# A streaming encoder layer on one Trainium2 core: seven block products for the first token group's last sixteen gate-up slabs

## The chip, the cores and the metric

One core of one Trainium2 chip runs the whole kernel as one program. The metric is the device time of one execution in microseconds; lower is better. Engines: TensorE (PE), VectorE (DVE), ScalarE (ACT), GpSimd (POOL), and SyncE (SP), which only issues DMAs here. ACT issues DMAs too.

## The reference, cut to what matters

One encoder layer is computed for 2048 prompt tokens and 32 sample tokens, D_MODEL = 1024, D_FF = 2816. The last part, which the change touches, is

```python
x = layer_norm(ALPHA * x + g1 * mix_out, ln1_g, ln1_b)
h = layer_norm(x) * (1.0 + sc2) + sh2
gu = h @ w_gu                                    # (tokens, 2 * D_FF)
ff = (silu(gu[..., :D_FF]) * gu[..., D_FF:]) @ w_down
x = layer_norm(ALPHA * x + g2 * ff, ln2_g, ln2_b)
```

Everything is float32. The kernel makes each float32 operand of these products from two float16 parts, a high and a low one, and sums three matmuls (high x high, high x low, low x high: `TERMS`).

## The kernel before, in words

The stages follow one another: projections, attention, the mixer's output (stage D, which leaves h in `hidden_t` as high and low halves), then stage E, gate-up and down. Stage E takes the tokens in three groups of 768, 768 and 544, and each group as two halves (384, 384, 272 columns). The 2816 hidden channels are 22 slabs (`NF`) of 128. For each slab j PE computes gate and up for both halves; ACT and DVE make silu(gate) * up; its high half is written by ACT, its low half by POOL, into `E_HID`. After 22 slabs come two down passes of three tiles of 128 tokens (`down`, line 2470 on).

**Groups two and three** compute a slab by seven block products (`product`, 2436 on; matmul line 2457). [gate; up] and the two halves of the 1024 input channels make a 2 x 2 block problem over the two token halves; with sums of weight blocks and sums of token blocks it takes 7 products of 12 matmuls, 84, in place of 8, 96. The results are combined by ACT (`copy1` to `copy3`, `sigmoid1`, `sigmoid2`, 1293 to 1322; high halves, 1327) and DVE (`gate1`, `gated1`, `up2`, `hidden2`, `hidden1`, 1928 to 1958). PE's order is 2, 6, 5, 7 of slab j, 1 of slab j + 1, 4 and 3 of slab j. Product 7 waits for the copy after 6, 4 for the copy after 7, 3 for `up2`. `copy2` waits for POOL's low half of the slab before, since its buffer holds the hidden part until then.

**Group one** (`gate_up`, 2413 on; matmul line 2426) computes each slab by plain products, 96 matmuls: blk 0 and blk 1, gate and up, 48 matmuls for each blk. Beside it, it prepares what groups two and three read:

- SP loads a slab of `w_gu` (1 MB float32) into one of two homes (`load_gu`, 688).
- ACT writes its high half (`gu_split`, 1264), DVE the low half (`gu_low`, 1878), into `E_GHL`.
- POOL makes four weight sums of 512 columns (`weight_sums`, 922 to 928) into `E_TSUM`; ACT and DVE split them (`sum_split`, 1272; `sum_low`, 1885) into `E_THL`, a single buffer.
- SP stores three blocks of 256 KB and the sums, 1 MB, to `gs_dram` (`store_gs`, 729 to 738), from where groups two and three load them.
- `hidden` (ACT 1282, 1284; DVE 1918, 1921; POOL's `lo_hid`, 942) makes the slab's hidden values, one blk after the other, with one float32 buffer `E_H` between them. PE's next slab waits for `hid_set` of the slab before, blk by blk.

Nothing is scheduled by a planner: each engine's order is written out by hand in its own loop over j, with semaphore waits. Slab 0's weights are split in stage D before its sums are due, so slab 0 is loaded and summed again in mid-stage as slab `NF` (`T_MID` = 11, `RAW_ORDER`). Two gate rows for the end (`gate_turn2`, 2467: PE; `gate_rows`, 1345: ACT) are made during slabs 1 and 2.

**Between the groups** POOL makes the next group's token sums (`token_sums`, 954 on, instructions at 964, 970, 972) while PE runs the down passes. In group one's first down pass ACT and DVE also split the 22 down slabs (`dn_split`, 1338; `dn_low`, 1964) and SP stores them one after the other (791), each store after the landing of the one before.

Of the kernel before, what the change touches and what calls it, by code (L numbers as in the profile page):

```python
# [57 lines left out]
def encoder_step(nc, x_prompt, x_sample, cache_k, cache_v, state_pool, c_prompt, c_sample,  # L58
# [5 lines left out]
    with ctx:  # L64
# [131 lines left out]
        E_GRAW = [w32(22576, 2048), w32(16896, 2048)]  # L196
# [153 lines left out]
        T_MID = NF // 2  # L350
        RAW_ORDER = [*range(T_MID + 1), NF, *range(T_MID + 1, NF)]
        RAW_POS = {m: at for at, m in enumerate(RAW_ORDER)}

        def graw_home(m):
            return E_GRAW[0 if m == 0 or RAW_POS[m] % 2 else 1]

        def raw_in(m):
            at = RAW_POS[m]
            home1 = at and at % 2 == 0
            return gu_raw[1 if home1 else 0], 32 * (at // 2 if home1 else (at + 3) // 2 if at else 1)  # L360

        def std_n(n):
            return 5 * n - 3 + 4 * (n > T_MID) if n else 1

        def sum_n(m, i):
            return (5 * T_MID + 2 if m == NF else 5 * m - 2 + 4 * (m > T_MID)) + i

        def stored_n(m):
            return 48 + 64 * (T_MID if m == NF else m) + 16 * (m > T_MID)

        ALL_STORED = 64 * NF

        GS_STEPS = [(1, 0)] + [(q, j + (q == 1)) for j in range(NF) for q in (2, 6, 5, 7, 1, 4, 3)
                               if (q, j) != (1, NF - 1)]
        MM_AT = (2 * NF, 9 * NF, 16 * NF)
        GS_MM = {key: at + 1 for at, key in enumerate(GS_STEPS)}

        def product_n(grp, q, j):
            return MM_AT[grp - 1] + GS_MM[q, j]

        def copy_n(grp, c, j):
            return 3 * NF * (grp - 1) + 3 * j + c

        def add_n(grp, a, j):
            return 2 * NF * (grp - 1) + 2 * j + a
# [78 lines left out]
        def _(sp):  # L464
# [39 lines left out]
            sp.dma_start(ln2_rows[:, 0, :], ln2_g[0:1, :].partition_broadcast(P)).then_inc(ln_in, 16)  # L504
            sp.dma_start(ln2_rows[:, 1, :], ln2_b[0:1, :].partition_broadcast(P)).then_inc(ln_in, 16)
# [191 lines left out]
            for t in range(14):  # L697
# [4 lines left out]
                if t == 12:  # L702
                    sp.wait_ge(gu_lo, 1)
                    load_gu(1)
# [11 lines left out]
            def next_gu(m):  # L716
                if m == 2:
                    sp.wait_ge(d_mm, NT + 1)
                    sp.wait_ge(d_x1, NT + 1)
                else:  # L720
                    gone = RAW_ORDER[RAW_POS[m] - 2]
                    if gone < NF:
                        sp.wait_ge(gu_lo, std_n(gone))
                    sp.wait_ge(t_sum, 4 * RAW_POS[gone])
                load_gu(m)
# [7 lines left out]
            def store_gs(m):  # L733
                sp.wait_ge(gu_lo, sum_n(m, 3))
                sp.wait_ge(gs_stored, stored_n(RAW_ORDER[RAW_POS[m] - 1]))
                if m < NF:
                    store_blocks(m)
                sp.dma_start(gs_dram[m % NF, :, 2:6], E_THL).then_inc(gs_stored, 16)

# [21 lines left out]
            for grp in range(3):  # L761
                n0, g0 = 6 * grp, 2 * NF * grp
                for c in range(NF):
                    if grp == 0:
                        if c == 0:
                            store_blocks(0)
                        if c + 2 < NF:
                            next_gu(c + 2)
                        if c + 2 == T_MID:
                            next_gu(NF)  # L770
                        if c + 1 < NF:
                            store_gs(c + 1)
                        if c + 1 == T_MID:
# [1777 lines left out]
```

## Time and profile before

| what | value |
| --- | --- |
| median of 3 runs | 2582.84 us (2579.41 to 2584.56) |
| the profiled execution | 2587.18 us, span 2585.5 us |
| PE, DVE, ACT, POOL busy | 94%, 55%, 39%, 35% |
| group one, gate-up | 1219.6 to 1575.5 us |
| group one, down | 1575.5 to 1755 us |
| group two, gate-up by seven products | 1755 to 2056 us |

A row of a group gives the engine, the source line, what is written and read with shapes, the count, the busy time, the mean duration, and the idle time of the engine just before with what ended it. In a timeline, each row begins with its start and its duration in microseconds from the start of the span.

### The profile page before, as it was taken

How to read it: one execution, taken by the hardware profiler on the slowest of the kernel's cores; microseconds unless marked ns; L12 is line 12 of the kernel's file. 1: busy time of each engine (PE TensorE's matmuls, PEld its weight loads, DVE VectorE, ACT ScalarE, POOL GpSimd, SP SyncE). 2: the span in 40 equal slices, each digit the busy share in tenths (PEclk: the TensorE clock that was granted, in tenths of full speed). 3: DMA queues.
4: the chain of work that ended last, by engine and by line, in shares of the span. 5: the costliest groups of instructions: out<-in, count | busy, mean ns of one | idle time of the engine just before them, and what ended most of it. 6: DMA issues, size and time to landing. Idle time of an engine off the chain costs nothing.

```text
span 2585.5 us, 36302 instructions
## 1 busy us (share of the span) xinstructions
PE 2431.2 (94%) x14328; PEld 1349.6 (52%) x14328; DVE 1415.9 (55%) x1861; ACT 1018.5 (39%) x1555; POOL 892.8 (35%) x1061
## 2 busy tenths in 40 slices
PE   4899899899998889999999999899999999999998
PEld 3445455444444444454565665345666544688733
DVE  4747665488888887889655554415333302433214
ACT  1522233499999895324443442102222200133200
POOL 1300000277777773333556556501111250111100
PEclk8899999899999999999999999999999999999999
DMA  7315868332332112222556566654454445476555
GB/s 249 100 50 171 283 235 272 120 99 82 99 84 81 34 66 93 78 94 84 165 179 212 179 198 234 227 196 155 155 163 131 139 138 180 153 224 203 186 164 167
DMA packets 216387, 395.63 MB, mean 153 GB/s; under 512 B 30189, under 2 KB 152365, under 8 KB 207642
## 3 DMA queue, kind: packets, MB, share of 16 engines
q1 hardware_dynamic: 199226, 331.45, 40.1%
q10 hardware_dynamic: 16992, 61.87, 7.7%
q8 instruction: 113, 1.85, 0.3%
q14 instruction: 56, 0.46, 0.1%
HBM read 302.97 MB, written 90.30 MB: 152 GB/s over the span
## 4 chain that ended last, share of the span: by engine, by line
PE 58%; DVE 9%; ACT 4%; POOL 4%; DMA 3%; issue 3%; SPq 0%; POOLq 0%; DVEq 0%; ACTq 0%
PE ps L2457 20%; PE ps L2497 15%; PE ps L2426 12%; PE ps L2361 3%; DMA dn_dram<-work 3%; DVE work L1709 3%; PE ps L2236 2%; POOL work L880 2%; PE ps L2213 2%; PE ps L2252 2%; ACT ps L1188 2%; ACT work L1176 2%; DVE work L1866 1%; DVE work L1706 1%; DVE work L1456 1%
## 5 line engine op out<-in xcount | busy, mean ns | idle before, releaser
L2457 PE MATMUL ps<-hidden_t,work 128*128 128x384 f16 (+1 forms) x3696 | 515.2, 303 | 1.9 <-ACT work L1307 1.1
L2497 PE MATMUL ps<-work 128*128 128x512 f16 x2244 | 472.5, 380 | 8.5 <-DVE work L1964 5.9
L2457 PEld LDWEIGHTS ps<-hidden_t,work 128*128 128x128 f16 x3696 | 361.4, 98 | 155.7 <-ACT work L1307 1.7
L2120 PE MATMUL ps<-hidden_t,work 128*128 128x416 f16 x1920 | 353.6, 345 | 14.2 <-DVE hidden_t L1474 10.0
L2426 PE MATMUL ps<-hidden_t,work 128*128 128x384 f16 x2112 | 347.6, 328 | 4.1 <-DVE work L1921 4.1
L2497 PEld LDWEIGHTS ps<-work 128*128 128x128 f16 x2244 | 206.4, 98 | 274.0 <-issue 29.8
L880 POOL TENSOR_TENSOR work<-work 128x512 f32<-128x512 f32 (+2 forms) x320 | 306.8, 965 | 112.4 <-DVE work L1709 63.9
L2426 PEld LDWEIGHTS ps<-hidden_t,work 128*128 128x128 f16 x2112 | 207.5, 98 | 144.3 <-issue 9.6
L2120 PEld LDWEIGHTS ps<-hidden_t,work 128*128 128x128 f16 x1920 | 190.3, 99 | 164.8 <-issue 17.8
L1709 DVE TENSOR_TENSOR_SCAN work<-ps,work 128x512 f32<-128x512 f32 x192 | 237.4, 1270 | 35.2 <-ACT ps L1188 34.3
L841 POOL TENSOR_TENSOR work<-work,col 128x1 f32<-128x1 f32 x68 | 33.2, 488 | 586.2 <-DVE work L1459 586.2
L949 POOL TENSOR_TENSOR work<-work 128x384 f16<-128x384 f32 (+1 forms) x88 | 75.2, 859 | 417.7 <-ACT work L1327 417.7
L2213 PE MATMUL ps<-work 128*128 128x512 f16 (+3 forms) x640 | 175.1, 357 | 37.3 <-DVE work L1709 29.5
L2236 PE MATMUL ps<-ident,work 128*128 128x128 f32 x1088 | 178.4, 280 | 21.8 <-POOL work L880 17.1
L1981 DVE TENSOR_TENSOR work<-ps,work 128x1024 f32<-128x1024 f32 (+1 forms) x17 | 20.8, 1223 | 311.6 <-PE ps L2497 310.3
L2236 PEld LDWEIGHTS ps<-ident,work 128*128 128x128 f32 x1088 | 131.8, 144 | 88.7 <-DVE work L1727 27.9
L1176 ACT ACTIVATE work<-ps,col 128x1024 f32<-128x1024 f32 (+1 forms) x160 | 165.2, 1032 | 8.4 <-PE ps L2213 6.8
L1188 ACT ACTIVATE ps<-ps,col 128x1024 f32<-128x1024 f32 (+1 forms) x160 | 161.5, 1009 | 2.1
L1199 ACT ACTIVATE work<-ps,col 128x512 f32<-128x512 f32 (+2 forms) x240 | 148.5, 619 | 32.6 <-PE ps L2236 29.5
L2252 PE MATMUL ps<-work 128*64 128x512 f32 (+3 forms) x640 | 159.8, 555 | 0.0
L2361 PE MATMUL ps<-work,hidden_t 128*128 128x512 f16 x720 | 159.4, 382 | 0.0
L1293 ACT ACTIVATE work<-ps 128x384 f32<-128x384 f32 (+1 forms) x44 | 19.5, 444 | 318.5 <-PE ps L2457 318.5
(243 smaller groups left out, 2723.5 us busy)
## 6 DMA issues: line engine op xcount, KB each, us to landing
work<-dn_dram ACTq DMA_DIRECT2D x96, 512.0 KB, 3.6
work<-gs_dram SPq DMA_DIRECT2D x88, 512.0 KB, 4.2
work<-gs_dram SPq DMA_DIRECT2D x44, 768.0 KB, 4.3
work<-in_w_ada SPq DMA_DIRECT2D x24, 1024.0 KB, 5.7
work<-in_w_gu SPq DMA_DIRECT2D x46, 512.0 KB, 7.1
work<-in_w_gu SPq DMA_DIRECT2D x22, 1024.0 KB, 5.9
gs_dram<-work SPq DMA_DIRECT2D x22, 1024.0 KB, 5.7
gs_dram<-work SPq DMA_DIRECT2D x66, 256.0 KB, 2.4
```

Source lines behind the costliest of these rows:

```text
L880: pool.tensor_tensor(a[:, 0:n], a[:, 0:n], PRJ[:, j, BLK * kc + 1:BLK * kc + n + 1], ALU.mult).then_inc(prod_set, 1)
L1176: act.activation(C_A[u % 3][:, j:j + 2, 0:n], ps[:, z:z + 2, 0:n], ACT.Sigmoid, scale=c1(C_Z + 2 * (h // 2) + 1)).then_inc(be_set, 1)
L1188: act.activation(ps[:, z:z + 2, 0:n], ps[:, z:z + 2, 0:n], ACT.Sigmoid, scale=c1(C_Z + 2 * (h // 2))).then_inc(sg_set, 1)
L1709: v.tensor_tensor_scan(row, ps[:, m % 4, w - 1::-1], row, PRJ[:, j, at + w:at + w + 1], ALU.mult, ALU.bypass).then_inc(scan_set, 1)
L2120: mm = pe.matmul(ps[:, blk, 0:PB], B_HL[s][:, wh * KD * P + k * P:wh * KD * P + (k + 1) * P], hidden_t[:, k, xh, PB * blk:PB * (blk + 1)], ...
L2213: mm = pe.matmul(ps[:, m % 4, 0:w], C_Q[e][:, qt:qt + P], C_K[e][:, half, BLK * kc:BLK * kc + w], start=(half == 0), stop=(half == 1))
L2236: mm = pe.transpose(ps[:, 4 + k % 2, j * P:(j + 1) * P], C_A[u % 3][:, j, kt * P:(kt + 1) * P], ident[:, :])
L2252: pe.matmul(ps[r:r + HD, 6 + b % 2, j0:BLK], C_V[e][:, 4 * kc + kt, :], C_AT[k % 4][:, j0:BLK], start=(kc == b and kt < 2), stop=(kc == 0 ...
L2361: mm = pe.matmul(ps[:, 2 * s + n, :], hidden_t[:, k, xh, tile_cols(t)], D_WO[k][:, wh, 512 * n:512 * (n + 1)], start=(k == 0 and (xh, wh) ...
L2426: mm = pe.matmul(ps[:, 2 * blk + w, 0:width], E_GHL[s][:, wh, w, k, :], hidden_t[:, k, xh, at:at + width], start=(k == 0 and (wh, xh) == ( ...
L2457: mm = pe.matmul(ps[:, bank, 0:n], E_GS[j % 2][:, GS_AT[q], wh, k, :], hidden_t[:, k0 + k, xh, at:at + n], start=(q in (1, 2, 5) and k == ...
L2497: mm = pe.matmul(ps[r:r + rows, 2 * slot + half, :], E_HID[:, j, xh, at:at + rows], E_DHL[slab_home(g)][:, wh, 512 * half:512 * (half + 1) ...
```

## The change

`CUT = 6`: group one computes slabs 0 to 5 plainly, and slabs 6 to 21 by seven products, each reading the weights where they are staged (`E_GHL`, `E_THL`) instead of from `gs_dram`. For that:

- The first group's token sums are made during slabs 1 to 4 (`first_sums`): POOL those of k = 0, 1, DVE those of k = 2, 3. Sums 1 to 3 go to buffers of their own (`E_S`), the fourth is kept in float32 (`E_S4`) and written over plain tokens after slab 5 (`last_sum`).
- `E_THL` becomes two buffers; sums 2 and 3 are made in place, in the raw weights' buffer, so they wait for the slab's low half.
- Slab 0's sums are made at once, two before and two after POOL's last-but-one low half of stage D. The repeated slab `NF` is gone. Slab 1's sums use the same buffer as slab 0's.
- In slabs 6 to 21 ACT, DVE and POOL do the seven-product steps of `product`'s other groups, with a slab's splits, low halves and sums in between.
- Gate rows are made in the down pass at slabs 2 and 6 (PE) and 6 and 10 (ACT); the two rows of the last norm are loaded after the x loads, ahead of the stores of the down slabs.
- Slab 0 and 1 of `w_gu` are loaded and split somewhat earlier in stage D.

The diff, cut to its core:

```diff
-        E_TSUM = [w32(at, 512) for at in (30768, 31280, 18944, 19456)]
-        E_THL = w16(28720, 4096).rearrange("p (q h n) -> p q h n", q=4, h=2)
+        E_TSUM = [w32(30768, 512), w32(31280, 512)]
+        E_THL = [w16(at, 4096).rearrange("p (q h n) -> p q h n", q=4, h=2) for at in (28720, 19968)]
...
+        CUT = 6
...
+        def sum_home(m, i):
+            return E_TSUM[i] if i < 2 else graw_home(m)[:, 512 * (4 - i):512 * (5 - i)]
...
@@ sync
                 if grp == 0:
-                    sp.wait_ge(gu_mm, 2 * NF)
+                    sp.wait_ge(gu_mm, MM_AT[1])
                     for n in range(3):
                         x1_in(n)
+                    sp.dma_start(ln2_rows[:, 0, :], ln2_g[0:1, :].partition_broadcast(P)).then_inc(ln_in, 16)
+                    sp.dma_start(ln2_rows[:, 1, :], ln2_b[0:1, :].partition_broadcast(P)).then_inc(ln_in, 16)
@@ gpsimd
                 else:
+                    pool.wait_ge(gu_lo, std_n(m))
...
+            pool.wait_ge(so_split, 1)
+            weight_sums(0, 0)
             lo_d(15, 1)
+            weight_sums(0, 1)
...
+                if part == 0:
+                    pool_step(x, part0(k, 1, 0), part0(k, 1, 1), ALU.add)
+                    pool_step(s1, part0(4 + k, 1, 0), part0(4 + k, 1, 1), ALU.add)
+                    pool_step(s1, x, s1, ALU.add)
+                    split(1, s1)
+                elif part == 1:
+                    pool_step(s2, part0(k, 0, 0), part0(k, 0, 1), ALU.add)
+                    pool_step(x, s2, x, ALU.subtract)
+                    split(3, x)
+                elif part == 2:
+                    pool_step(s2, s1, s2, ALU.subtract)
+                    split(2, s2)
+                else:
+                    pool_step(s1, part0(4 + k, 0, 0), part0(4 + k, 0, 1), ALU.add)
+                    pool_step(E_S4[k], s1, s2, ALU.subtract)
...
+                    if grp == 0 and j < CUT:
+                        if j:
                             weight_sums(j + 1, 0)
+                        if 1 <= j <= 4:
+                            if j == 1:
+                                first_turned()
+                            first_sums((j - 1) // 2, 2 * (j - 1) % 4)
                         lo_hid(grp, j, 0)
+                        if j:
                             weight_sums(j + 1, 1)
+                        if 1 <= j <= 4:
+                            first_sums((j - 1) // 2, 2 * (j - 1) % 4 + 1)
                         lo_hid(grp, j, 1)
...
+                    elif grp == 0:
+                        if j > CUT:
+                            lo_half(0, j - 1, 1)
+                            lo_half(0, j - 1, 0)
+                        weight_sums(j + 1, 0)
+                        weight_sums(j + 1, 1)
@@ scalar
+                elif m == 1 and pair == 0:
+                    act.wait_ge(gs_stored, stored_n(0))
...
+            copy1(0, CUT)
+            for j in range(CUT, NF):
+                if j + 1 < NF:
+                    gu_split(j + 1, (j + 1) % 2, product_n(0, 3, j - 1) if j > CUT else 2 * CUT)
...
+                if j > CUT:
+                    high_half(0, j - 1, 0)
+                sigmoid1(0, j)
+                copy2(0, j)
                 if j + 1 < NF:
                     sum_split(j + 1, 0)
...
+                copy3(0, j)
+                if j + 1 < NF:
+                    sum_split(j + 1, 1)
+                    copy1(0, j + 1)
...
+                sigmoid2(0, j)
+                high_half(0, j, 1)
+            high_half(0, NF - 1, 0)
@@ vector
+                    if grp == 0 and j < CUT:
+                        if j:
                             gu_low(j + 1, (j + 1) % 2)
+                        if 1 <= j <= 4:
...
+                            first_sums(2 + (j - 1) // 2, 2 * (j - 1) % 4)
                         hidden(0, j, 0)
+                        sum_low(j + 1 if j else 0, 0)
+                        if 1 <= j <= 4:
+                            first_sums(2 + (j - 1) // 2, 2 * (j - 1) % 4 + 1)
                         hidden(0, j, 1)
+                        sum_low(j + 1 if j else 0, 1)
                         if j == 0:
+                            sum_low(1, 0)
+                            sum_low(1, 1)
...
+                    if grp == 0:
+                        gate1(0, j)
+                        if j + 1 < NF:
+                            gu_low(j + 1, (j + 1) % 2)
+                        gated1(0, j)
+                        if j + 1 < NF:
+                            sum_low(j + 1, 0)
...
+                        up2(0, j)
+                        if j + 1 < NF:
+                            sum_low(j + 1, 1)
...
+                        hidden2(0, j)
+                        hidden1(0, j)
@@ tensor
                 if grp == 0:
-                    for j in range(NF):
+                    for j in range(CUT):
                         gate_up(grp, j)
-                        if j in (1, 2):
-                            gate_turn2(j - 1)
...
+                for q, j in GS_STEPS[grp]:
+                    product(grp, q, j)
```

## Rows read from the trace of the kernel before

**Rows 1.** The page: time of the engines, one DMA issue.
```profile
PE 2431.2 (94%) x14328; PEld 1349.6 (52%) x14328; DVE 1415.9 (55%) x1861; ACT 1018.5 (39%) x1555; POOL 892.8 (35%) x1061
...
gs_dram<-work SPq DMA_DIRECT2D x22, 1024.0 KB, 5.7
```

**Rows 2.** Windows: length; PE, PEld, DVE, ACT, POOL busy; clock; DMA share; GB/s.
```profile
1219.00:1575.00 356.00, 350.53 (x2142) 210.53 (x2142) 206.52 (x219) 152.25 (x218) 197.10 (x140) 0.99 0.59 183
1575.00:1672.00 97.00, 90.09 (x413) 39.36 (x410) 39.11 (x27) 23.86 (x22) 67.83 (x66) 1.00 0.72 242
```

**Rows 3.** Windows of one plain slab and of one seven-product slab.
```profile
1450.91:1466.51 15.60, 15.60 (x98) 9.39 (x97) 8.92 (x9) 6.66 (x9) 8.81 (x6) 1.00 0.59 185
1901.62:1915.27 13.65, 13.65 (x86) 8.22 (x85) 4.88 (x7) 3.72 (x8) 1.83 (x2) 1.00 0.52 174
```

**Rows 4.** Timeline of all engines in a plain slab, DVE and POOL.
```profile
1449.47 0.74 DVE L1885 SCALAR_TENSOR_TENSOR work<-work,col 128x512 f16<-128x512 f32 x1
...
1455.70 1.30 POOL L922 TENSOR_TENSOR work<-work 128x512 f32<-128x512 f32 x1 [1.35 <-DVE work L1885]
...
1456.51 2.64 DVE L1878 SCALAR_TENSOR_TENSOR work<-work,col 128x2048 f16<-128x2048 f32 x1 [0.95 <-ACT work L1264]
...
1457.08 3.22 POOL L924 TENSOR_TENSOR work<-work 128x512 f32<-128x512 f32 x1
```

**Rows 5.** Timeline of DVE and POOL near the stage's start.
```profile
1244.98 1.10 DVE L1885 SCALAR_TENSOR_TENSOR work<-work,col 128x512 f16<-128x512 f32 x1 [5.91 <-ACT work L1272]
1245.49 1.36 POOL L942 TENSOR_TENSOR work<-work 128x384 f16<-128x384 f32 x1
...
1247.33 0.60 DVE L1918 SCALAR_TENSOR_TENSOR work<-ps,col,work 128x384 f32<-128x384 f32 x1
```

**Rows 6.** Groups of DVE by shape in the second group's seven-product slabs.
```profile
L1958 DVE SCALAR_TENSOR_TENSOR work<-work,col 128x384 f32<-128x384 f32 x18 | 23.5, 1304 | 0.6
...
L1950 DVE SCALAR_TENSOR_TENSOR work<-work,col 128x384 f32<-128x384 f32 x17 | 10.5, 619 | 0.6
```

**Rows 7.** DVE's groups by shape in stage D: instructions without POOL beside them.
```profile
L1878 DVE SCALAR_TENSOR_TENSOR work<-work,col 128x2048 f16<-128x2048 f32 x2 | 4.6, 2298 | 0.0
...
L1827 DVE TENSOR_TENSOR hidden_t<-work,hidden_t 128x128 f16<-128x128 f32 x1 | 0.3, 293 | 0.0
L1826 DVE CAST hidden_t<-work 128x128 f16<-128x128 f32 x1 | 0.2, 227 | 0.0
```

**Rows 8.** Timeline of POOL in the second group's token sums.
```profile
1583.87 0.50 POOL L970 CAST hidden_t<-work 128x384 f16<-128x384 f32 x1
1584.45 0.92 POOL L972 TENSOR_TENSOR hidden_t<-work,hidden_t 128x384 f16<-128x384 f32 x1
1585.33 0.91 POOL L964 TENSOR_TENSOR work<-hidden_t 128x384 f32<-128x384 f16 x1
1586.32 1.00 POOL L964 TENSOR_TENSOR work<-work 128x384 f32<-128x384 f32 x1
```

**Rows 9.** Timeline of PE from slab 1 on, with the first round of ACT and DVE.
```profile
1239.21 17.44 PE L2426 MATMUL ps<-hidden_t,work 128*128 128x384 f16 x96 [0.59 <-DVE work L1921]
...
1250.42 1.99 ACT L1264 ACTIVATE work<-work,col 128x2048 f16<-128x2048 f32 x1
...
1252.51 2.92 DVE L1878 SCALAR_TENSOR_TENSOR work<-work,col 128x2048 f16<-128x2048 f32 x1 [0.60 <-ACT work L1264]
...
1256.48 1.04 PE L2467 MATMUL ps<-ident,mod_t 128*128 128x128 f32 x8
1257.36 15.76 PE L2426 MATMUL ps<-hidden_t,work 128*128 128x384 f16 x96
...
1417.89 2.40 PE L2426 MATMUL ps<-hidden_t,work 128*128 128x384 f16 x7 [3.50 <-DVE work L1921]
```

**Rows 10.** Timeline of PE in the first down pass.
```profile
1623.84 8.00 PE L2497 MATMUL ps<-work 128*128 128x512 f16 x36 [1.39 <-DVE work L1964]
```

**Rows 11.** Windows around slab 0's end.
```profile
1240.00:1246.00 6.00, 6.00 (x29) 3.21 (x27) 1.02 (x1) 3.34 (x10) 3.62 (x4) 0.72 0.31 86
```

More of the change, by code:

```diff
@@ L375, in encoder_step, with thl_home, first_slab, steps_from @@
-        MM_AT = (2 * NF, 9 * NF, 16 * NF)
-        GS_MM = {key: at + 1 for at, key in enumerate(GS_STEPS)}
+        def thl_home(m):
+            return E_THL[m % 2 if m else 1]
+        def sum_home(m, i):
+            return E_TSUM[i] if i < 2 else graw_home(m)[:, 512 * (4 - i):512 * (5 - i)]
+        def first_slab(grp):
+            return 0 if grp else CUT
+        def steps_from(first):
+            return [(1, first)] + [(q, j + (q == 1)) for j in range(first, NF) for q in (2, 6, 5, 7, 1, 4, 3)
+                                   if (q, j) != (1, NF - 1)]
@@ L950, in lo_half, with part0, first_sums, pool_step @@
                                    ALU.subtract).then_inc(hid_lo, 1)
+            def part0(k, side, hl):
+                return hidden_t[:, k, hl, 384 * side:384 * side + 384]
+            def first_sums(k, part):
+                x, s1, s2 = E_SF[0:3]
+                def pool_step(out, a, b, op):
+                    own.done(pool.tensor_tensor(out, a, b, op))
+                    own.wait()
+                def split(q, full):
+                    own.done(pool.tensor_copy(E_S[q][:, k, 0, :], full))
+                    own.wait()
+                    own.done(pool.tensor_tensor(E_S[q][:, k, 1, :], full, E_S[q][:, k, 0, :], ALU.subtract))
+                    own.wait()
+                if part == 0:
[10 more added lines that the diff above has]
+                    split(2, s2)
+                else:
+                    pool_step(s1, part0(4 + k, 0, 0), part0(4 + k, 0, 1), ALU.add)
+                    pool_step(E_S4[k], s1, s2, ALU.subtract)
+            def first_turned():
+                pool.wait_ge(d_hi, NT + 1)
+                pool.wait_ge(d_mm, NT + 1)
+                pool.wait_ge(d_xhat, NT + 1)
+                pool.wait_ge(x1_stored[0], 144)
+                pool.wait_ge(x1_stored[1], 128)
+            def last_sum(k):
+                own.done(pool.tensor_copy(part0(k, 1, 0), E_S4[k]))
+                own.wait()
+                own.done(pool.tensor_tensor(part0(k, 1, 1), E_S4[k], part0(k, 1, 0), ALU.subtract))
             def rstd_e(n):
@@ L1414, in _ @@
                 dn_split(g)
+                if g in (6, 10):
+                    gate_rows(g // 4 - 1)
             for g in range(NF, 2 * NF):
@@ L2484, in down @@
                         pe.wait_ge(*DN_IN[g])
+                    if p == 0 and i == 0 and j in (2, 6):
+                        gate_turn2(j // 4)
                     if j == 0:
```

308 lines of the change are left out of this document (184 added, 124 removed).

## The prediction

> **What bounds the kernel now.** I read the page first: TensorE (PE) is busy for 94% of the span [rows 1]. Then the windows of the stage that is changed: from 1219 to 1575 us, the gate-up of the first token group, PE is busy 350.5 of 356 us; VectorE (DVE) and GpSimd (POOL) both work for a little over half of it [rows 2]. So PE sets this stage, and the reader should see why seven products instead of eight look like a gain. The windows of one slab give the price: a standard slab (96 matmuls of 384 columns) takes 15.60 us, a seven-product slab of the second group (84) takes 13.65 [rows 3]. Both are full of PE work. The gain on offer is 1.95 us a slab, 16 x 1.95 = 31.2 us.
>
> The third view, instructions in order of time, shows what those windows hide: DVE and POOL hinder each other. POOL's first weight sums take 1.27 to 1.30 us, but the one issued at 1457.08 takes 3.22. DVE had begun the low half of the weights at 1456.51, waited for POOL's sum to end at 1457.00, ran to 1459.15, and POOL finished 1.15 us after that [rows 4]. Where both have short instructions they alternate: from 1244.98 a DVE instruction of 0.74 us takes 1.10 and POOL's low half, 0.92 elsewhere, takes 1.36, each beginning in truth where the other ends (the pattern comes once more until 1248.5); a DVE instruction that reads PSUM (line 1918) then runs beside POOL in its usual 0.60 [rows 5]. In group two the last multiply of a slab, all in SBUF, takes 1.30 against 0.62 when POOL's low half starts just before it [rows 6]. I therefore count one resource that is on no engine's line, the SBUF access that POOL and a DVE instruction with two SBUF operands can't have together. For it the durations of both engines add up.
>
> **The change part by part.** The sum starts from the profiled execution, 2587.18 us (span 2585.5); the median of the runs, 2582.84, is 4.3 lower.
>
> The load of that resource, per slab. POOL: four weight sums at 1.28 and two low halves at 0.92, 6.96 us. DVE: the slab's low half, 2.30 alone [rows 7], and four sum low halves at 0.74 [rows 4], 5.26 us. Together 12.2 of the 15.60 us: that fits today. The change keeps all of it in every slab and adds to it twice.
>
> First, the token sums in slabs 2 to 5 (rounds j = 1 to 4). For one k: 14 instructions on POOL, from the same work in the second group's token sums: 4 x 0.91 + 4 x 1.00 + 3 casts at 0.50 + 3 x 0.92 = 11.9 us [rows 8]. On DVE the rows have no such instruction of 384 columns; 128 columns take 0.29 and 0.23 us [rows 7], and a line from the 0.29 to the 0.74 of 512 columns gives 0.59, the cast between 0.36 and 0.49, so 11 x 0.59 + 3 x 0.42 = 7.7 us. Two k each: 23.8 + 15.4 = 39.2. With the four rounds' own 48.9 and some 0.04 us between steps that wait for their predecessor (80 steps, 3 us) it comes to 91 us for four rounds that PE would do in 62.4. PE can't run ahead: slab j + 1 needs its weights' low half and the hidden parts of slab j, which stand behind these steps in DVE's order. Cost **+29 us**. Bounds: +6 if DVE's plain additions didn't take the shared access (the rows show it only for the multiply forms with two SBUF operands, lines 1878, 1885, 1958), 0 if nothing were shared, and +35 if handovers cost twice as much.
>
> The Trainium skill has a rule for this ("SBUF — State Buffer", Who interferes with whom): a DVE instruction with two SBUF inputs, tensor_tensor too, and a GpSimd instruction that reads SBUF exclude each other for a whole instruction. By it the 29 stands, by the narrowest reading of the rows it would be 6.
>
> Second, the opening. Slab 0's sums now come ahead of slab 1's, and both use one buffer, so ScalarE (ACT) may write slab 1's only when slab 0's 1 MB store has landed (5.7 us [rows 1]). Before, ACT split slab 2 in 1.99 us, round 1 began on DVE at 1252.5, and PE began slab 2 at 1257.36 [rows 9]. Now: POOL has four more sums before slab 0's are split, the last low half comes near 1249, the store lands near 1254.7, four splits take 2.6, the split of slab 2 takes 2.0, so DVE's round 1 begins near 1261: **+8.5 us**. Behind ACT's wait are queued hidden part (1, 0) and the weights of slab 2, and PE waits for both. The extra gate work that was here goes: PE's two turns (0.9 each between slabs [rows 9]) move to the down-projection, where PE waits anyway: **-1.8**. The repeated sums of slab 0 in mid-stage go, and with them PE's 3.5 us wait at 1417.9 [rows 9]: **-3.5**.
>
> Third, the change-over at slab 6. The last token sums (two k on POOL at 1.42 us, two on DVE), the low part of slab 5 and the copy of product 1 come one after the other: half 1 set (2.5 us after PE's end), high, low, copy, 4.1 us against the 3.9 of two products; then ACT does the split of slab 7, and POOL is some 3 us late into its weight sums. Slab 6 and its start need from 6 to 13 us more than a steady slab; I take **+9**, since round 5 has 3.4 us of slack.
>
> Fourth, the product slabs. ACT, busy for 152 of the 356 us today [rows 2], stays off the limit. The shared access has POOL's 6.96 and DVE's 2.30 + 4 x 0.74 + three multiplies at 0.62 [rows 6] = 7.1: **14.1 us, over the 13.65**. That is the floor. On top, nobody uses the access while the order allows only PSUM reads: the second half's gate multiply and the gate addition (0.6 each, as line 1918 [rows 5]), and some eight handovers between engines, together 0.6 as an estimate. The chain closes: POOL's fourth sum, its split on ACT, copy of the next product 1 behind it, sigmoid, hidden 2, high half, weight split, hidden 1's low half on POOL behind the 2.3 us of the weights, copy 2, product 7. That adds to 15.9 us a slab, 16.4 if no instruction overlaps the next one's start. I take 15.9, 0.3 over the standard slab: 16 x 0.3 = **+5**. PE waits about 2.3 us in each slab, most before product 7. The ends: 14.1 (-24 us) and 13.65 (-31).
>
> Fifth, the down-projection. Two 512 KB loads of the last norm's rows now stand in SP's queue between the x loads and the first store of down weights; those stores set this stage (PE waits for DVE's low halves from 1623.8 on [rows 10]). At least their issue, 0.9 us, at most their traffic, 1 MB at about 240 GB/s [rows 2], 4 us: **+1**. Two gate rows on ACT (1.0 each) hide in its waits for the stores; without those they would cost 2.
>
> Sum: 29 + 8.5 - 1.8 - 3.5 + 9 + 5 + 1 = **+47**, 2634 on the profiled execution's scale, **2630 us** against the median.
>
> **The rivals.**
> A, the other side: PE stays the bound. If the shared access matters only for long instructions, or the order leaves slack that I counted as full, the product slabs run at 13.65 (-31.2), the waits of -5.3 go, and the opening costs about 4: 2583 - 33 = 2550. It decides at the product slab: below 15.3 us a slab with first slabs hidden. For it speaks that both engines are idle 40% of the time in today's stage; against it the alternation of short instructions [rows 5]. Chance 0.13.
> B: DVE's additions don't take the shared access: +6 in place of +29, 2607. Chance 0.14.
> C: the product slabs reach their floor, 14.1: 29 us less than with 15.9, 2601. Chance 0.11.
> D: PE's clock. After PE sat idle near 1237 the granted clock was 0.72 from 1240 to 1246 [rows 11] (between 1.2 and 2.4 GHz), and slab 1 took 17.44 us in place of 15.60 [rows 9]. If every slab's wait of 2.3 us does that within the chain, up to 1.8 x 16 = 29 more: 2659. Against it: most of such a loss falls into PE's slack. Chance 0.13.
>
> **How the numbers follow.** My own forecast has 0.46, D 0.13, B 0.14, C 0.11, A 0.13; 0.03 is left for a result within 0.2% (5 us), about what a measurement of this kernel can tell from no change: several mild errors at once. Faster 0.13, same 0.03, slower 0.84. The range takes in C and B below, and D above: 2596 to 2664.
>
> **What would show it.** PE's first matmul of slab 2 near 1270, not 1257; the start of the products near 1363, not 1320; 15.9 us between the seventh products of two slabs with a 2 us gap before each, released by ACT's copy; POOL's casts and additions of the first token sums stretched by DVE and the reverse, both busy nearly all of slabs 2 to 5; PE's busy time down by about 31 us while the stage grows from 356 to about 402. I am wrong if product slabs take 13.7 us with no gaps, or if DVE's additions stay at 0.6 us beside POOL's.

## The result and the profile after

The changed kernel takes 2602.01 us (median of 4 runs, 2600.03 to 2606.98), the kernel before 2581.33 in the same session (2579.41 to 2584.56): ratio 1.007 [1.0057, 1.0083], 21 us slower. The forecast had the direction and was more than twice too large (+47). The two profiled executions stand 16.4 us apart (spans 2601.9 and 2585.5), and the account below is made against those 16.4; executions of one kernel differ by some microseconds, many of them ahead of the changed stage, so stages are measured from PE's first gate-up matmul or from slab 1.

The page after, engines' busy time and the store whose landing ACT waits for (before: [rows 1]):

```profile
PE 2406.9 (93%) x14136; PEld 1329.8 (51%) x14136; DVE 1502.0 (58%) x1943; ACT 1037.6 (40%) x1603; POOL 951.5 (37%) x1095
...
gs_dram<-work SPq DMA_DIRECT2D x22, 1024.0 KB, 6.8
```

PE does 24 us less work and the kernel is slower: PE no longer sets the stage. Windows of the stage, of slabs 2 to 5 as a whole, of slab 5, and of one steady product slab (length; PE, PEld, DVE, ACT, POOL busy; clock; DMA share; GB/s; before: [rows 2, 3]):

```profile
1220.02:1590.45 370.43, 325.06 (x1937) 190.25 (x1937) 290.71 (x300) 170.85 (x265) 252.81 (x173) 0.96 0.51 173
1268.78:1351.28 82.50, 70.91 (x384) 39.91 (x385) 70.75 (x61) 26.93 (x39) 64.16 (x49) 0.89 0.38 127
1333.14:1351.28 18.14, 18.14 (x96) 10.25 (x97) 14.54 (x13) 7.96 (x12) 12.32 (x10) 0.86 0.39 130
1451.88:1466.63 14.75, 13.81 (x84) 8.14 (x85) 11.39 (x12) 7.94 (x12) 10.09 (x7) 1.00 0.58 202
```

The stage took 355.9 us before and takes 370.4. In it PE's busy time fell by 25.4 us, and its idle time rose from 5.5 to 45.4. The timeline of PE shows where (start, length, lines, the idle time before it and its releaser; before: [rows 9]):

```profile
1237.59 15.76 PE L2598 MATMUL ps<-hidden_t,work 128*128 128x384 f16 x96 [0.32 <-DVE work L2066]
1268.78 18.06 PE L2598 MATMUL ps<-hidden_t,work 128*128 128x384 f16 x96 [15.43 <-DVE work L2066]
1289.95 17.44 PE L2598 MATMUL ps<-hidden_t,work 128*128 128x384 f16 x96 [3.11 <-DVE work L2066]
1311.69 9.30 PE L2598 MATMUL ps<-hidden_t,work 128*128 128x384 f16 x48 [4.30 <-DVE work L2066]
...
1333.14 18.30 PE L2598 MATMUL ps<-hidden_t,work 128*128 128x384 f16 x96 [3.86 <-DVE work L2066]
1351.28 4.06 PE L2647 MATMUL ps<-hidden_t,work 128*128 128x384 f16 x24
...
1451.88 2.11 PE L2647 MATMUL ps<-ln_rows,work 128*128 128x384 f16 x12 [1.00 <-ACT work L1392]
...
1466.63 2.11 PE L2647 MATMUL ps<-ln_rows,work 128*128 128x384 f16 x12 [0.94 <-ACT work L1392]
...
1590.45 7.93 PE L2686 MATMUL ps<-work 128*128 128x512 f16 x36
```

The waits of slabs 2 to 5 end with DVE's hidden part (line 2066), which stands behind the token sums; the granted clock is lower there, 0.89 over the four slabs. The product slabs follow each other in 14.77 us (1451.88 to 1466.63 here), with one wait of 1 us before the seventh product. Set against the kernel before, the 16.4 us are made of four parts: slab 2 starts 11.0 us later after the first gate-up (48.8 against 37.8); slabs 2 to 5 take 82.5 in place of 63.2, +19.3; from the start of slab 6 to the down-projection it is 239.2 in place of 254.9 (1320.6 to 1575.5), -15.7 (1320.6 is 1273.83 and three slabs of 15.6); the down-projection, 181.2 us against 179.7, adds 1.5. The sum is 16.1.

SP's store of slab 0's sums, and ACT, DVE and POOL in the first of the four rounds, in order of time:

```profile
1248.85 0.34 SPq L752 DMA_DIRECT2D gs_dram<-work  x1
...
1254.12 2.56 ACT L1362 ACTIVATE work<-work,col 128x512 f16<-128x512 f32 x4 [7.29 <-DMA gs_dram<-work]
...
1258.77 3.16 DVE L1992 SCALAR_TENSOR_TENSOR work<-work,col 128x2048 f16<-128x2048 f32 x1
...
1261.85 1.26 DVE L2014 TENSOR_TENSOR work<-hidden_t 128x384 f32<-128x384 f16 x1
...
1263.15 1.15 DVE L2015 TENSOR_TENSOR work<-hidden_t 128x384 f32<-128x384 f16 x1
1263.96 1.19 POOL L978 TENSOR_TENSOR work<-work 128x384 f32<-128x384 f32 x1
...
1267.36 0.62 DVE L2063 SCALAR_TENSOR_TENSOR work<-ps,col,work 128x384 f32<-128x384 f32 x1
...
1269.33 0.92 POOL L961 TENSOR_TENSOR work<-work 128x384 f16<-128x384 f32 x1 [2.42 <-ACT work L1374]
1269.84 2.63 DVE L2000 SCALAR_TENSOR_TENSOR work<-work,col 128x512 f16<-128x512 f32 x2 [1.20 <-ACT work L1362]
```

DVE's additions take 1.15 to 1.26 us beside POOL's, not the 0.59 that the prediction gave them alone: they do take the shared access. The last two lines are waits that the prediction did not count: POOL waits 2.42 us for ACT's high half, which waits for DVE's hidden part (1.24 us the next time), and so the access stands unused between two full stretches. DVE too is idle for 10.8 us in slabs 2 to 5, in nine waits of 1.2 such as this one, each for ACT's split of the weight sums, which stands behind that high half. No wait of another engine ends with PE between the start of slab 2 and the start of slab 6, so the lower clock of these slabs only shortened PE's own waits.

### The profile page after: what moved, and what is told of

Its sections match the earlier page's. It is cut to its first block, busy times and chain, and to the rows that moved or that the text cites. A ratio compares the mean times of both kernels' runs of the same rounds, so it can differ in the third digit from the quotient of the medians.

```text
span 2601.9 us, 36208 instructions
## 1 busy us (share of the span) xinstructions
PE 2406.9 (93%) x14136; PEld 1329.8 (51%) x14136; DVE 1502.0 (58%) x1943; ACT 1037.6 (40%) x1603; POOL 951.5 (37%) x1095
## 4 chain that ended last, share of the span: by engine, by line
PE 46%; DVE 13%; POOL 9%; ACT 5%; issue 5%; DMA 3%; SPq 0%; POOLq 0%; DVEq 0%; ACTq 0%
PE ps L2647 20%; PE ps L2686 15%; PE ps L2533 3%; DMA dn_dram<-work 3%; DVE work L1823 3%; PE ps L2408 2%; POOL work L968 2%; POOL work L893 2%; PE ps L2385 2%; PE ps L2424 2%; ACT ps L1273 2%; ACT work L1261 2%; DVE work L2000 1%; DVE work L1980 1%; POOL work L937 1%
## 5 line engine op out<-in xcount | busy, mean ns | idle before, releaser
L2647 PE MATMUL ps<-hidden_t,work 128*128 128x384 f16 (+1 forms) x4464 | 642.8, 307 | 2.5 <-ACT work L1399 1.7
L2647 PEld LDWEIGHTS ps<-hidden_t,work 128*128 128x128 f16 x4464 | 436.4, 98 | 206.3 <-ACT work L1399 1.7
L968 POOL TENSOR_TENSOR work<-work 128x384 f16<-128x384 f32 (+1 forms) x120 | 134.0, 1121 | 497.5 <-ACT work L1424 497.5
L2292 PEld LDWEIGHTS ps<-hidden_t,work 128*128 128x128 f16 x1920 | 189.8, 99 | 162.7 <-issue 16.9
L1823 DVE TENSOR_TENSOR_SCAN work<-ps,work 128x512 f32<-128x512 f32 x192 | 237.4, 1270 | 35.0 <-ACT ps L1273 34.0
L2126 DVE TENSOR_TENSOR work<-ps,work 128x1024 f32<-128x1024 f32 (+1 forms) x17 | 20.8, 1223 | 311.4 <-PE ps L2686 310.4
L1284 ACT ACTIVATE work<-ps,col 128x512 f32<-128x512 f32 (+2 forms) x240 | 148.2, 618 | 33.9 <-PE ps L2408 30.6
L1385 ACT ACTIVATE work<-ps 128x384 f32<-128x384 f32 (+1 forms) x60 | 27.0, 451 | 318.7 <-PE ps L2647 318.7
L2000 DVE SCALAR_TENSOR_TENSOR work<-work,col 128x512 f16<-128x512 f32 x88 | 103.5, 1192 | 56.8 <-ACT work L1362 56.8
L859 POOL PARTITION_ALL_REDUCE small<-small x15 | 5.3, 352 | 340.2 <-DVE small L1566 340.2
```

The source lines that it names most:

```text
L968: pool.tensor_tensor(E_HID[:, j, 1, cols:cols + n], full, E_HID[:, j, 0, cols:cols + n], ALU.subtract).then_inc(hid_lo, 1)
L1823: v.tensor_tensor_scan(row, ps[:, m % 4, w - 1::-1], row, PRJ[:, j, at + w:at + w + 1], ALU.mult, ALU.bypass).then_inc(scan_set, 1)
L2292: mm = pe.matmul(ps[:, blk, 0:PB], B_HL[s][:, wh * KD * P + k * P:wh * KD * P + (k + 1) * P], hidden_t[:, k, xh, PB * blk:PB * (blk + 1)], ...
L2647: mm = pe.matmul(ps[:, bank, 0:n], w, x, start=(q in (1, 2, 5) and k == 0 and (wh, xh) == (0, 0)), stop=(k == 3 and (wh, xh) == TERMS[-1]) ...
```

## The experiments

**Without the first group's token sums.** Both engines leave the sums of rounds 1 to 4 out and zero their buffers once, in round 1, where the first sums stood; the three products that read these sums multiply zeros. Left out: the calls `first_sums(...)` on POOL and DVE.

> The changed kernel without the first group's token sums on both engines (their buffers are set to zero once in round 1, so slabs 6 to 21 multiply zeros in three of seven products; the work of all else is unchanged). My theory, shared SBUF access between POOL and DVE: slabs 2 to 5 take PE near 15.7 us each instead of 20.6, the products start some 20 us earlier than at 1351.3, the product slabs stay at 14.8, the whole is 19 to 22 us below the changed kernel, so within 5 us of the kernel before. Rival 1, PE's clock after each gap is what costs: the same, since the gaps go too, but then PE's busy time in slabs 2 to 5 must fall by as much as the stage. Rival 2, the queue order alone (the sums stand ahead of the hidden part, no conflict): about 7.7 us a round on DVE alone would hide in 15.6, so little is gained, under 8 us.

Measured: 2583.22 us, ratio to the kernel before 0.9995 [0.9986, 1.0005]. PE from slab 1 on:

```profile
1234.52 15.76 PE L2603 MATMUL ps<-hidden_t,work 128*128 128x384 f16 x96 [0.46 <-DVE work L2069]
1264.04 63.85 PE L2603 MATMUL ps<-hidden_t,work 128*128 128x384 f16 x384 [13.76 <-DVE work L2069]
```

Slabs 2 to 5 run without a gap, and the whole loss is gone: about 20 us, although PE still waits 13.8 us for slab 2 and the product slabs still take 14.8. The clock as the only cause (rival 1) is out: PE's busy time in slabs 2 to 5 fell by 7 us, the stretch by 18.6. The 20 us are a lower bound for the sums, because zeroing the buffers keeps DVE busy for 3.7 us (1258.90 to 1262.58) ahead of the hidden part for which slab 2 waits. The fifth experiment, where DVE does neither, shows what stands there.

**POOL's share alone.** DVE's calls left out and its buffers zeroed, POOL's kept.

> Only DVE's share of the first group's token sums is left out (its buffers are zero), POOL's stays. Shared access: POOL's additions go back from 1.2 to 0.91 and 1.00 us, casts to 0.50, and rounds 1 to 4 fall from 21.4 to between 16 and 18 us, the first and third longer than the second and fourth. Rival, each engine limited by its own queue only: POOL's instructions keep their durations, and the rounds fall to what POOL's own work is, 15.0 us or less, hidden behind PE's 15.6.

Measured once, without an interval: 2582.71 us; slabs 2 to 5 in one piece of 64.04 us, 16.0 a slab, the lower edge of the 16 to 18 expected. 6 us of sums a round on POOL cost nothing here, though POOL is busy for 61.3 of 63.9 us. Its additions for the sums fell from a mean of 1.7 us to between 1.2 and 1.4, and not to the 0.91 and 1.00 expected, since DVE's other steps still stretch them. DVE's share alone was not run, so that only both shares together overfill is shown from POOL's side.

**The high half first.** On ACT, in the product slabs:

```diff
+                if j > CUT:
+                    high_half(0, j - 1, 0)
                 if j + 1 < NF:
                     gu_split(j + 1, (j + 1) % 2, product_n(0, 3, j - 1) if j > CUT else 2 * CUT)
...
-                if j > CUT:
-                    high_half(0, j - 1, 0)
```

> One swap on ACT in slabs 7 to 21: the high half of the hidden part (21 ns to 0.5 us of work) comes ahead of the 2 us weight split, so POOL's low half of it can start before DVE's 2.3 us weight low half takes the access, and the second copy no longer waits for it. Theory that the 14.78 us of a product slab come from this chain of waits: the 0.95 us gap before product 7 goes and a slab takes 13.7 to 14.1, the whole 10 to 16 us less than the changed kernel. Rival, the access is full (my floor of 14.1 us from summed durations): the slab stays above 14.4 and the gap moves to another product, under 6 us gained.

Measured: 2594.07 us, ratio 1.0041 [1.0028, 1.0055], 8 us less than the changed kernel, where 10 to 16 were expected. Changed kernel first, this one second, the engines around the seventh product:

```profile
1446.01 1.99 ACT L1349 ACTIVATE work<-work,col 128x2048 f16<-128x2048 f32 x1
...
1447.90 0.51 ACT L1424 ACTIVATE work<-work 128x384 f16<-128x384 f32 x1
1448.03 2.35 DVE L1992 SCALAR_TENSOR_TENSOR work<-work,col 128x2048 f16<-128x2048 f32 x1 [0.46 <-ACT work L1349]
...
1448.49 2.67 POOL L968 TENSOR_TENSOR work<-work 128x384 f16<-128x384 f32 x1 [1.04 <-ACT work L1424]
...
1451.12 1.57 POOL L937 TENSOR_TENSOR work<-work 128x512 f32<-128x512 f32 x1
1451.25 0.49 ACT L1392 ACTIVATE work<-ps 128x384 f32<-128x384 f32 x1 [2.33 <-POOL work L968]
...
1455.68 1.72 POOL L944 TENSOR_TENSOR work<-work 128x512 f32<-128x512 f32 x1
```

```profile
1401.29 2.11 PE L2647 MATMUL ps<-ln_rows,work 128*128 128x384 f16 x12
...
1407.41 1.40 DVE L2000 SCALAR_TENSOR_TENSOR work<-work,col 128x512 f16<-128x512 f32 x2
...
1407.54 4.07 PE L2647 MATMUL ps<-hidden_t,work 128*128 128x384 f16 x24 [0.24 <-DVE work L2086]
1411.45 4.06 PE L2647 MATMUL ps<-work 128*128 128x384 f16 x24
```

In the changed kernel the high half (1424) stands behind the 2 us split, so POOL's low half falls behind DVE's 2.35 us and takes 2.67 in place of 0.92, and ACT's copy waits for it. With the two lines exchanged that gap is gone, one of 0.24 us comes before product 3, and a slab takes 14.06 us (1397.39 to 1411.45). One order decided 0.7 us a slab.

**The opening.** Slab 2's split and hidden part (1, 0) ahead of slab 1's sums, on ACT and DVE:

```diff
@@ scalar
+                    if j == 1:
+                        sum_split(1, 0)
+                        sum_split(1, 1)
                     sum_split(j + 1, 0)
...
                     sum_split(0, 1)
-                    sum_split(1, 0)
-                    sum_split(1, 1)
```

> On ACT and DVE, slab 2's weight split and the hidden part (1, 0) come ahead of slab 1's sum splits, so that they no longer stand behind ACT's 7.3 us wait for the landing of slab 0's sums. Theory, the opening is that queued wait: PE starts slab 2 near 1258 instead of 1268.8, but the sums of round 1 still fill the access, so only 5 to 8 us of it reach the start of the products. Rival, the opening is the access too (four extra weight sums and slab 1's sums in a row): slab 2 starts after 1264 and under 3 us are gained in the whole.

Measured: 2597.77 us, ratio 1.0055 [1.004, 1.007]. PE waits 5.05 us for slab 2 in place of 15.43, and slab 2 starts 20.8 us after slab 1 and not 31.2. Later waits (2.79, 3.14, 6.18 and 3.86 us) take a part back: the products start 107.5 us after slab 1 in place of 113.7, and the time falls by 4, a little less than the 5 to 8 expected.

**The sums spread over POOL alone.** `CUT = 10`, the sums of all four k on POOL in rounds 1 to 8, none on DVE.

> All of the first group's token sums on POOL, one k in two rounds, rounds 1 to 8, and the seven products from slab 10 on (CUT = 10) instead of 6; DVE makes none. The result is complete. Theory, only POOL and DVE sums together overfill the shared access (POOL's alone hid behind PE): slabs 2 to 9 take PE 15.7 us each with no waits after the opening, product slabs stay at 14.8. Against the changed kernel: 20 us of waits gone, 4 product slabs fewer at 0.8 each, +3: some 15 to 19 us less, 1 to 5 us over the kernel before. Rival, the total work on the access decides wherever it stands: 24 us of additions more on POOL than in the run without DVE's share brings the waits back, over 8 us of PE waits in slabs 3 to 9.

Measured: 2590.58 us, ratio 1.0019 [1.001, 1.0028]. PE from slab 2 on, and the window of two later slabs:

```profile
1266.13 72.83 PE L2596 MATMUL ps<-hidden_t,work 128*128 128x384 f16 x432 [9.62 <-DVE work L2066]
```

```profile
1349.26:1383.12 33.86, 31.54 (x193) 18.63 (x193) 17.89 (x18) 13.47 (x19) 32.64 (x27) 1.00 0.50 171
```

For four and a half slabs PE has no gap; then POOL, busy for 32.6 of 33.9 us, is itself the bound, at 16.93 us a slab (PE's waits add up to 4.7 us). The four rounds of the second experiment were hidden because POOL could fall behind for that long. The prediction's sum of durations would give such a round 12.2 + 23.8 / 4 = 18.2 us, more than the 16.93 measured.

This run also shows what the sums did to the opening. With nothing on DVE ahead of the hidden part, slab 2 starts 25.4 us after slab 1 (1240.74) and not 31.2, so 5.8 us of the changed kernel's wait for slab 2 belong to the first token sums.

**That with the high half first and the new opening.**

> The kernel of e5 with the two order changes of e3 (high half before the weight split) and e4 (slab 2's split and hidden part before slab 1's sums). If the three causes are separate, they add: product slabs at 14.1 (12 x 0.7 = 8 us), the opening's 13.8 us wait of PE mostly gone (8 to 11 us): 2563 to 2573 us, 10 to 18 us below the kernel before. If the opening only moves the wait to the sums, as it did in part in e4, 2572 to 2578.

Measured: 2583.63 us, ratio 0.9992 [0.9983, 1.0]. A miss: ten plain slabs forgo four product slabs, and the later plain ones still take 16.93 us (1337.72 to 1371.57 holds two).

**The access by itself.** Behind the end of the kernel before, POOL and DVE run additions of 384 columns and steps of 512 with two SBUF operands, first alone, then together; then POOL beside DVE additions with a PSUM operand, and beside DVE casts.

> The kernel before with a short contest after its last result: POOL and DVE alone and together, independent instructions on their own buffers (8 each alone; 16 each together: additions of 384 columns on both; 512 columns, addition on POOL and the two-operand multiply-subtract on DVE; DVE addition with one PSUM operand beside POOL; DVE cast beside POOL). If each instruction holds the access for its whole duration, a pair of 384 costs 1.0 + 0.59 = 1.6 us and a pair of 512 1.27 + 0.74 = 2.0. If it holds it only while it streams, with its start and end outside, a pair costs less: about 1.2 and 1.7, as the changed kernel's rows suggest. With a PSUM operand neither is stretched. The cast: stretched if DVE's fast form also takes the access.

Timelines of POOL and of DVE in that part (start, time of all, count); 1024 and 2092 are plain additions, 2096 the multiply form, 2109 has the PSUM operand, 2112 is the cast:

```profile
2591.68 7.63 POOL L1024 TENSOR_TENSOR work<-work 128x384 f32<-128x384 f32 x8 [3.42 <-DVE small L2086]
2603.55 9.79 POOL L1024 TENSOR_TENSOR work<-work 128x512 f32<-128x512 f32 x8 [4.08 <-DVE small L2086]
2619.12 20.24 POOL L1024 TENSOR_TENSOR work<-work 128x384 f32<-128x384 f32 x16 [5.63 <-DVE small L2086]
2639.48 26.28 POOL L1024 TENSOR_TENSOR work<-work 128x512 f32<-128x512 f32 x16
2666.52 15.26 POOL L1024 TENSOR_TENSOR work<-work 128x384 f32<-128x384 f32 x16 [0.60 <-DVE small L2086]
2681.89 16.99 POOL L1024 TENSOR_TENSOR work<-work 128x384 f32<-128x384 f32 x16
```

```profile
2599.50 3.84 DVE L2092 TENSOR_TENSOR work<-work 128x384 f32<-128x384 f32 x8 [7.97 <-POOL col L1026]
2613.53 5.39 DVE L2096 SCALAR_TENSOR_TENSOR work<-work,col 128x512 f32<-128x512 f32 x8 [10.06 <-POOL col L1026]
...
2619.43 19.08 DVE L2092 TENSOR_TENSOR work<-work 128x384 f32<-128x384 f32 x15
...
2666.82 7.05 DVE L2109 TENSOR_TENSOR work<-ps,work 128x384 f32<-128x384 f32 x15
...
2681.97 17.13 DVE L2112 CAST work<-work 128x384 f16<-128x384 f32 x16 [7.97 <-POOL col L1026]
```

Alone, one addition of 384 columns takes 0.95 us on POOL (7.63 / 8) and 0.48 on DVE (3.84 / 8). Together they alternate, one of each every 1.27 us (20.24 / 16). By the durations that the prediction added up, 1.00 and 0.59, it would be 1.59: the method overstates a pair by a quarter. At 512 columns a pair takes 1.64 (26.28 / 16) against 1.28 + 0.74 = 2.02. With a PSUM operand neither is slowed (0.95 and 0.47). A cast beside POOL's additions takes 1.07 each.

**The sums behind the hidden part.** All of the changed kernel's work, `CUT = 6`, in another order in rounds 1 to 4, on both engines (DVE shown):

```diff
+                        hidden(0, j, 0)
+                        if 1 <= j <= 4:
                             first_sums(2 + (j - 1) // 2, 2 * (j - 1) % 4)
-                        hidden(0, j, 0)
```

> The changed kernel with one difference: in rounds 1 to 4 the token sums come after the hidden part and its low half, on both engines, not ahead of them. Shared access theory: the work on the access is the same, so the rounds keep about 21 us and at most the last half round is gained, 2 to 6 us in the whole. Rival, only the place in the order costs (PE waits because the hidden part stands behind the sums): rounds fall to 16 to 17 us and 15 us or more are gained.

Measured: 2591.02 us, ratio 1.0019 [1.001, 1.0029], 11 us less by the medians and 13 by the ratios. Slabs 2 to 5:

```profile
1261.10:1335.48 74.38, 67.66 (x384) 38.78 (x385) 71.75 (x66) 28.24 (x39) 71.37 (x53) 0.93 0.43 145
```

The same instructions take 74.4 us in place of 82.5. POOL is busy for 71.4 of 74.4, where it was busy for 64.2 of 82.5: ACT gets DVE's hidden part before the sums, so POOL's low half is ready when POOL comes to it, and DVE's waits for ACT's split of the weight sums shrink from 10.8 to 1.4 us. Slab 2 also starts 5.5 us sooner after slab 1. The gain lies between the two expectations: in the two traces, 8.1 + 5.5 us of the 25 that the sums cost (worked out below), more than half, was their place.

**The three orders together, and without the opening.** Sums behind the hidden part and high half first (second label), and the opening added (first label).

> Three orders changed together, nothing left out: the first token sums after the hidden part on both engines, the high half ahead of the weight split on ACT, and slab 2's split and hidden part ahead of slab 1's sums. If the three gains are of three different waits they add: order of the sums 11 us, high half 8 us, opening 4 us, so about 23 us below the changed kernel's 2602, or 2577 to 2582 and a ratio to the kernel before of 0.996 to 0.998. If the work of DVE and POOL in slabs 2 to 5 sets the time whatever its order, the opening gives nothing more, and the time is the same as without it, about 2583 (ratio 0.999).

> The same without the opening's new order. If the gains add, 19 us below the changed kernel, about 2583 and a ratio of 0.999, some 4 us above the kernel with all three. If the opening gives nothing once the sums stand after the hidden part, the two agree within 1 us.

Measured: 2577.58 us with all three, ratio **0.9974 [0.9965, 0.9984]**; 2581.14 without the opening, 0.9982 [0.9974, 0.9991]. By the ratios the three had given 0.0029, 0.0015 and 0.0051 singly; taken from 1.0070 that is 0.9975. The gains add within the intervals, as those of three different waits do. This kernel computes the same and beats both. PE in it:

```profile
1236.40 15.76 PE L2602 MATMUL ps<-hidden_t,work 128*128 128x384 f16 x96 [0.20 <-DVE work L2068]
1254.70 9.64 PE L2602 MATMUL ps<-hidden_t,work 128*128 128x384 f16 x48 [2.54 <-DVE work L2068]
...
1333.69 4.06 PE L2651 MATMUL ps<-hidden_t,work 128*128 128x384 f16 x24
...
1394.60 4.07 PE L2651 MATMUL ps<-hidden_t,work 128*128 128x384 f16 x24 [0.22 <-DVE work L2088]
...
1563.92 7.93 PE L2690 MATMUL ps<-work 128*128 128x512 f16 x36
```

**More load in the product slabs.** To the best kernel, POOL gets 2 (then 4) additions of 384 columns behind the weight sums of ten product slabs, their results unused.

> The best kernel so far (sums after the hidden part, high half first, new opening; 2577.6) with two more additions of 384 columns on POOL behind the weight sums in each of ten product slabs (j = 7 to 16), their results unused. If the SBUF access is full in a product slab, as the prediction's 14.1 us say against the 14.06 measured, each addition lengthens the slab by its duration: 2 x 1.0 x 10 = 20 us, 2597. If the sum of durations overstates the access by the fifth that the separate contest of two queues showed (1.27 in place of 1.54 us for a pair), the load is about 11.6 and becomes 13.2, still below PE's 13.7: no more than 3 us, under 2581.

> The same with four more additions in each of the ten slabs. By full durations 4 x 1.0 x 10 = 40 us, 2617. By the corrected load 11.6 + 3.3 = 14.9 against slabs of 14.06: about 8 us, 2586, and more only if POOL's low halves come late behind the additions (POOL is idle for 4.2 us there).

Measured: 2585.70 us with two, ratio 0.9999 [0.999, 1.0008], and 2586.29 with four, 1.0002 [0.9993, 1.0011]: by the ratios 6.5 and 7 us over the best kernel, not 20 and 40. Neither of the two expectations for two additions holds (2597, or under 2581). The one for four names 2586, but by a sum that gave two additions at most 3 us, so its match is luck. A slab with four:

```profile
1424.47 4.92 POOL L1091 TENSOR_TENSOR work<-work 128x384 f32<-128x384 f32 x4
...
1425.45 2.08 DVE L2006 SCALAR_TENSOR_TENSOR work<-work,col 128x512 f16<-128x512 f32 x2
...
1425.59 4.08 PE L2655 MATMUL ps<-hidden_t,work 128*128 128x384 f16 x24 [0.91 <-DVE work L2092]
...
1440.27 2.94 PE L2655 MATMUL ps<-hidden_t,work 128*128 128x384 f16 x17 [0.86 <-DVE work L2092]
```

Both have slabs of 14.7 us (product 3 from 1425.59 to 1440.27), 0.7 over the 14.0 of the best kernel. By these rows the first two additions meet DVE's last two splits of the weight sums, which take 2.08 us (at 1425.45, the same with two additions) in place of 1.40 (at 1394.47 in the best kernel; 1407.41 above is the same pair). Behind these two stand the hidden part, its halves and POOL's next weight sums, so the 0.68 us pass into every slab; the later additions fall where DVE reads PSUM or where POOL would wait. So the access is not full in a product slab: a third and a fourth addition cost nothing that can be measured. What an addition costs depends on whom it holds up.

## Why the prediction was right and wrong, by its steps

**Direction, mechanism, places: right.** PE's slab 2 was forecast near 1270 and came at 1268.78 (the first product, forecast near 1363, where the prediction's own terms give 1320.6 + 35.7 = 1356, came at 1351.28); the wait before every seventh product, released by ACT's copy, is there; DVE's additions share the access with POOL's; PE's busy time fell by 25 us and not by 31, since slabs 2 to 5 held 7.7 us more at the lower clock (70.9 against 63.2), and the stage grew. Leaving the sums out takes the loss away (2583.22). By the rule of the Trainium skill ("SBUF — State Buffer", Who interferes with whom), a DVE tensor_tensor with both inputs in SBUF and a GpSimd instruction that reads SBUF exclude each other; the runs agree on who is held up: 0.48 us alone, 1.27 beside POOL, 0.47 with a PSUM operand. They do not bear out an exclusion for a whole instruction as the profile times it: a pair takes 1.27 us and not 0.95 + 0.48 = 1.43. Rival B (+6 for the sums), which gave DVE's additions a free path, is refuted by that, though its 2607 lies near the result.

**The opening: +8.5 less one gate turn, +7.6; measured about +5.** The mechanism was right and its steps nearly so: slab 0's store was forecast to land near 1254.7, and ACT went on 5.3 us after its issue, at 1254.1. The forecast's own terms (2.6 and 2.0 us behind the landing) add to 1259.3 and not to "near 1261"; DVE's round 1 began at 1258.8, after PE's first gate-up 5.8 us later than before, and the gate turn that went gave back 0.8. PE's slab 2, though, started 11.0 us later: the other 5.9 are the first token sums, which stand ahead of the hidden part on DVE (1261.85 to 1267.33), and they belong to the next term. The two kernels without sums there (the fifth experiment and the one with the sums behind the hidden part) have slab 2 25.4 and 25.7 us after slab 1, not 31.2.

**The four rounds: +29 less the other turn, +28; measured about +25,** 5.9 in the wait for slab 2 and 19.3 in slabs 2 to 5. The failing step is "for it the durations of both engines add up". The forecast round was 22.75 us (91 / 4); the measured starts lie 21.2, 21.7 and 21.5 apart, and the last slab, with no wait behind it, took 18.1. The near match in the middle is partly luck. The true load is lower: the same work in another order took 18.6 us a slab (74.38 / 4), and an estimate with the contest's pair (22.0 us of durations a round, 12.2 + 39.2 / 4, by 1.27 / 1.59) gives 17.6. The order is worse than taken for: sums ahead of the hidden part leave POOL waiting 2.4 and 1.2 us in a round, and DVE 1.2 twice. Two errors, of opposite sign. The lower clock, 70.9 us of PE work against 63.9 in one piece without the sums, is no third one: no wait of another engine ended with PE in that stretch, and the 2.4 us more of the last slab shortened the wait behind it, which DVE ended.

**The product slabs: +5, measured -13.3** (16 x (14.77 - 15.60)). This is the largest error, 18 of the 31 us between 47 and 16.4. The step that failed is "that adds to 15.9 us a slab": the chain and its last wait were the right ones (the exchange of two lines on ACT removes it), but PE waits 1.0 us and not 2.3. In the trace the chain is 6.3 us for POOL's four weight sums (1451.12 to 1457.40), 5.8 from there to POOL's next delayed low half (1463.24) and 2.7 for that, 14.8 together; the prediction gives only the total of its steps, so which of them is 1.1 us too long stays open. And 14.1, the load of the access by durations, is not a measure of it: with two additions more and with four a slab took 14.7 us. That the exchanged order reached 14.06 is then no confirmation of that sum; there PE is busy for 13.8. Rival C has its time near the result, but not its mechanism for the whole.

**Change-over +9, measured about +3** (239.2 - 16 x 14.77 = 2.9). PE waits 1.99 us twice there, where the forecast, from steps added up, had 6 to 13 us. **Mid-stage: -3.5, measured about -5.3** (254.9 - 16 x 15.60): besides PE's wait, the ten slabs behind it took 157.8 us in one piece, 1.8 more than ten times 15.60. **Down-projection: +1, measured +1.5.**

**Rival D** (the clock, +29 over the product slabs) did not occur: the window of a product slab shows 1.00, with waits of 1 us. Behind waits of 3.1 to 4.3 us in slabs 2 to 5 it was lower, 0.86 in slab 5, between the two levels of 1.2 and 2.4 GHz. **Rival A** (PE stays the bound, faster) fails for the kernel as changed, but with three orders turned round it comes out on its side of zero, 2577.6, by 7 us and not by 33: slabs of 14.0 and the first rounds still cost.

## What to carry to other kernels

When two engines share an access, the sum of their durations is too high, here by a quarter for a pair, and not a price: take the period of a pair from a measurement with both queues full, and check which of the two is waiting for a third engine before calling the access full. Work that is added between a result and its consumer is to be put behind the hand-off, not ahead of it; here the same instructions in another order were worth 11 us (13 by the ratios), and the three orders together turned a loss of 0.7% into a gain of 0.26%. A share that hides in four rounds can be the bound in eight, so test a cover over the whole length for which it is used.

## What the runs showed of the hardware

- DVE and POOL additions of 384 columns, both in SBUF, alternate at 1.27 us a pair, against 1.43 by their own spacings alone (0.95 + 0.48): a part of each is outside the shared access. DVE's cast from float32 to float16 in SBUF, with one input, is slowed too: 1.07 us each beside POOL's additions, whose own spacing rises from 0.95 to 1.06. The contest has no cast alone; in the changed kernel the same cast took 0.54 us at 1265.59, at the end of a cast of POOL's.
- The durations of POOL's instructions are longer than their spacing: the eight lone additions have a mean of 991 ns and come every 0.95 us. The Trainium skill ("Perfetto Trace Analysis", GPSIMD Engine Instruction) says to time them by the spacing of their starts; the runs agree, though the difference is only 4%.
- Waits of 1 us in each product slab left the granted clock at 1.00. Behind waits of 3.1 to 4.3 us in slabs 2 to 5 of the changed kernel the slabs took 17.3 to 18.3 us, but not always: in the kernel with the new opening the slab behind a wait of 3.14 us took 15.76, the one behind 6.18 took 17.59.
